# The first three experts of the last pass held in SBUF and loaded in the key pass, with their value chunks split there

## The reference

```
def block(hb):
    qh = (hb @ w_q).reshape(tb, PEER_HEADS, 2, PEER_HALF)
    ...
    best, pos = lax.top_k(cand, PEER_TOPK)
    eidx = jnp.take_along_axis(cidx, pos, axis=-1)
    gates = jax.nn.softmax(best.astype(jnp.float32), axis=-1).astype(hb.dtype)
    act = jax.nn.gelu(jnp.einsum('td,thkd->thk', hb, u_tab[eidx]), approximate=False)
    return jnp.einsum('thk,thkd->td', gates * act, v_tab[eidx])
...
x = x + gt2 * _peer(h2, ...)
return _rmsnorm_2(x, final_norm_w)
```

## Time and profile before

| | us |
|---|---|
| median of 3 runs | 2736.82 |
| lowest, highest | 2735.11, 2752.26 |
| profiled execution | 2736.22 |
| its span | 2734.4 |
| PE busy | 2642.6 (97%) |
| DVE busy | 1921.7 (70%) |
| POOL busy | 1311.6 (48%) |
| ACT busy | 1067.2 (39%) |
| DMA moved | 539.31 MB, mean 197 GB/s |
| key pass in `weigh` | about 1860 to 2171.5 |
| last pass | 2186.9 to 2722 |

### The profile page before, as it was taken

One profiled execution on the slowest core, in us unless ns is written; L12 is line 12 of the kernel. 1 busy time (PEld: TensorE's weight loads), 2 busy tenths in 40 slices (PEclk: granted clock), 3 DMA queues, 4 the chain that ended last, 5 costly groups with the idle time before them and its releaser, 6 DMA issues. The chain is left out here.

```text
span 2734.4 us, 37662 instructions
## 1 busy us (share of the span) xinstructions
PE 2642.6 (97%) x13717; PEld 2229.8 (82%) x13717; DVE 1921.7 (70%) x3096; ACT 1067.2 (39%) x1703; POOL 1311.6 (48%) x622
## 2 busy tenths in 40 slices
PE   8999999999899999999999999999999799999997
PEld 6888887665788887878777899999999788888885
DVE  5445242787854447599776387768999689888897
ACT  4322321455342323352223233335666544444443
POOL 4444452211444445454124467782323368877883
PEclk9999999999999999999899999999999999999998
DMA  5444342112334444332012265558999999999994
GB/s 194 146 143 145 106 166 62 56 54 74 104 123 154 146 138 153 101 110 67 16 63 87 83 179 163 166 157 338 401 392 389 373 359 386 384 385 387 386 387 168
DMA packets 190912, 539.31 MB, mean 197 GB/s; under 512 B 14416, under 2 KB 96464, under 8 KB 170704
## 3 DMA queue, kind: packets, MB, share of 16 engines
q1 hardware_dynamic: 88688, 306.23, 33.6%
q0 software_dynamic: 18432, 134.23, 12.2%
q10 hardware_dynamic: 83680, 97.46, 10.3%
HBM read 482.28 MB, written 55.57 MB: 197 GB/s over the span
## 5 line engine op out<-in xcount | busy, mean ns | idle before, releaser
L358 POOL TENSOR_TENSOR ring_low<-ring,ring_high 128x1024 fp32r<-128x1024 f32 x323 | 801.3, 2482 | 984.4 <-ACT ring_high L318 979.7
L318 ACT ACTIVATE ring_high<-ring 128x1024 fp32r<-128x1024 f32 x354 | 374.2, 1057 | 617.9 <-PE ps L415 485.4
L413 PE MATMUL ps<-u,ring_high 128*128 128x512 f32 (+1 forms) x1504 | 565.8, 376 | 19.6 <-DVE u L520 10.0
L414 PE MATMUL ps<-u,ring_high 128*128 128x512 f32 (+1 forms) x1504 | 559.9, 372 | 0.0
L415 PE MATMUL ps<-u,ring_low 128*128 128x512 f32 (+1 forms) x1504 | 559.7, 372 | 0.0
L358 POOL TENSOR_TENSOR ring_low_more<-ring,ring_high_more 128x1024 fp32r<-128x1024 f32 x103 | 266.8, 2593 | 153.6 <-ACT ring_high_more L318 152.8
L413 PEld LDWEIGHTS ps<-u,ring_high 128*128 128x128 f32 x1504 | 284.0, 189 | 63.4 <-POOL ring_low L641 10.0
L414 PEld LDWEIGHTS ps<-u,ring_high 128*128 128x128 f32 x1504 | 284.2, 189 | 40.1 <-issue 1.4
L415 PEld LDWEIGHTS ps<-u,ring_low 128*128 128x128 f32 x1504 | 284.0, 189 | 39.3
L2867 POOL DMA_INDIRECT fetched_rows<-in_peer_uv,fetch_index x128 | 157.4, 1230 | 180.1 <-DVE ps L2887 138.1
L3487 DVE TENSOR_TENSOR expert_product<-group_acts,group_weights 128x384 f32<-128x384 f32 x128 | 162.9, 1273 | 70.0 <-issue 50.8
(11 more groups left out here) (476 smaller groups left out, 5269.8 us busy)
## 6 DMA issues: line engine op xcount, KB each, us to landing
ring<-in_peer_u SPq DMA_DIRECT2D x128, 512.0 KB
ring<-in_peer_uv SPq DMA_DIRECT2D x128, 512.0 KB
ring<-in_ffn_gu SPq DMA_DIRECT2D x88, 512.0 KB
ada_weights<-in_ada_w SPq DMA_DIRECT2D x48, 512.0 KB, 3.9
ring<-in_ffn_down SPq DMA_DIRECT2D x48, 512.0 KB
expert_acts<-kept_acts ACTq DMA_DIRECT2D x128, 192.0 KB
expert_weights<-weight_stage ACTq DMA_DIRECT2D x24, 1024.0 KB
group_acts<-expert_acts ACTq DMA_DIRECT2D x15, 1536.0 KB
```

The source lines that it names most:

```text
L318: act.activation(k.highs[p], k.ring[:, s], ACT.Copy).then_inc(k.high_ready[p].sem, 1)
L358: pool.tensor_tensor(k.lows[p], k.ring[:, s], k.highs[p].bitcast(F32), ALU.subtract)\
L413: pe.matmul(out, k.highs[p][:, w], high, start=first, stop=False)
L414: pe.matmul(out, k.highs[p][:, w], low, start=False, stop=False)
```

## The change

It makes a class `Edge` for the experts 0, 1 and 2 of the last pass (`EDGE` is now 3). Their activations (3 x 1536 bytes per partition) and gates (24 blocks x 3 experts x 16 tokens) have a place of their own in SBUF at byte 220096, a multiple of 64, where the later products, high and low halves of `combine` lie afterwards. SP loads them in the key pass: the activations and blocks 0 to 17 in front of key chunk 4 of the last round, blocks 18 to 21 behind the first four value chunks; blocks 22 and 23 are copied by ACT out of `weight_stage`. The first four value chunks are all split in the key pass, the low halves on DVE and not on POOL. Products 0 and 1, the rounding of product 0 and its rest also stand in `weigh`. Group 0 without those three experts is loaded in two steps, experts 3 and 4 (semaphore `second`), then 5 to 7. PE's wait for the banks of the key pass is made explicit, per pair of banks. Group 1 is loaded after rounding 3 and not after rounding 1.

```diff
-EDGE = 2
+EDGE = 3
+SECOND = 5
...
+class Edge:
+    AT = 220096
+    SOON = NB - 6
+    def __init__(self, k, ctx, x):
...
+        self.acts = k.nc.alloc_sbuf_tensor_at("edge_acts", [P, EDGE, DT], F32, offset=self.AT)
+        self.weights = k.nc.alloc_sbuf_tensor_at("edge_weights", [P, NB, EDGE * WT], F32, offset=self.AT + EDGE * unit)
...
+    def load_blocks(self, k, sp, lo, hi):
+        for slot in range(2):
+            sp.wait_ge(self.x.staged[slot].sem, 16 * ((hi + 1 - slot) // 2))
+        sp.dma_start(self.weights[:, lo:hi], k.dram["expert_weights"][lo:hi, :, 0:EDGE].rearrange("b p e t -> p b (e t)"))\
+          .then_inc(self.loaded.sem, 16)
+    def load(self, k, sp):
+        for s in range(EDGE):
+            sp.wait_ge(self.x.stored[s].sem, 16)
+        sp.dma_start(self.acts[:], k.dram["expert_acts"][0:EDGE].rearrange("e p t -> p e t")).then_inc(self.loaded.sem, 16)
+        self.load_blocks(k, sp, 0, self.SOON)
+    def copy(self, act):
...
+        for slot in range(2):
+            copy = act.activation(self.weights[:, NB - 2 + slot].rearrange("p (e t) -> p e t", t=WT),
+                                  x.stage[:, slot, 0:EDGE], ACT.Copy)
+    def first(self, dve, n):
+        if n == 0:
+            for b in range(2):
+                dve.wait_ge(self.x.weighed[b].sem, NB)
+            dve.wait_ge(self.loaded.sem, 48)
+            dve.wait_ge(self.copied.sem, 1)
+        if n == 2:
+            dve.wait_ge(self.product_ready.sem, 2)
+        self.multiply(dve, n, self.acts[:, n], self.weights[:, :, n * WT:(n + 1) * WT])
...
 def weigh
-            stream.load(sp)
+            stream.load(sp, midway=lambda: edge.load(k, sp))
+            edge.load_blocks(k, sp, edge.SOON, NB - 2)
...
+                if i == U_ITERS - 1 and e == 6:
+                    edge.copy(act)
...
+                if i == U_ITERS - 1 and e >= 5:
+                    stream.split_high(act, U_ITERS, e - 4)
+                if i == U_ITERS - 1 and e == 6:
+                    edge.round(act, 0)
...
+            edge.first(dve, 0)
+            edge.first(dve, 1)
+            edge.rest(dve, 0)
+            low(8 * U_ITERS + 2)
+            low(8 * U_ITERS + 3)
...
 def combine
-            load_weights(sp, 0, NB - 1, 0, 8, weights_loaded[0])
-            load_acts(sp, 0, 0, EDGE, first_acts)
-            load_acts(sp, 0, EDGE, 8, acts_loaded[0])
+            load_weights(sp, 0, NB - 1, EDGE, SECOND, second)
+            load_acts(sp, 0, EDGE, SECOND, second)
+            load_weights(sp, 0, NB - 1, SECOND, 8, weights_loaded[0])
+            load_acts(sp, 0, SECOND, 8, acts_loaded[0])
...
-                if n == 1:
+                if n == EDGE:
                     for s in range(ACTS):
                         act.wait_ge(x.stored[s].sem, 16 * (P // ACTS))
                     load_acts(act, 1, 0, 8, acts_loaded[1])
```

More of the change, by code:

```diff
@@ L303, in load @@
                     beside(i)
+        if midway is not None:
+            midway()
         for j in range(SLOTS, self.n):
@@ L3206, in v_place, with weigh @@
     return V_PLACES[c - PER_U * U_ITERS]
-def weigh(k, x, choices, acts, block):
+def weigh(k, x, choices, acts, edge, block):
     nc = k.nc
@@ L3429, in coef_high @@
             def coef_high(n):
-                act.wait_ge(product_ready.sem, n + 1)
-                act.activation(high[:, n % WIDE], product[:, n % 3], ACT.Copy).then_inc(high_ready.sem, 1)
+                edge.round(act, n)
                 g = n // 8 + 2
-                if n == 1:
+                if n == EDGE:
                     for s in range(ACTS):
@@ L3451, in _ @@
             copy.then_inc(last_block.sem, 1)
[L3452 to L3455 removed]
+            coef_high(3)
             for n in range(P - WIDE):
@@ L3494, in _ @@
                         x.take_row(dve, c)
-            split(P - 1)
+            edge.rest(dve, P - 1)
             for c in range(CHOICES - 2, CHOICES):
```

104 lines of the change are left out of this document (67 added, 37 removed).

## The result

| | before | after |
|---|---|---|
| median, us | 2735.84 (20 runs, 2728.99 to 2752.26) | 2745.47 (20 runs, 2738.14 to 2753.16) |
| profiled execution | 2736.22, span 2734.4 | 2738.14, span 2736.4 |
| PE busy | 2642.6 | 2656.9 |

The ratio is 1.0033, 95% interval 1.0025 to 1.0042: 9.6 us slower, where 2732.0 and a range to 2742 were forecast. The profiled execution of the changed kernel is the lowest of its 20. It is read first; a second profile of the same kernel, among the experiments, is a usual one.

The account below looks back on a forecast made before the run. The prediction took the DMA engines, through the last group's load, to set the end. Its terms, -1.3 + 1.0 - 3.0 - 1.0 = -4.3 us, took 2736.2 to 2731.9, stated as 2732, with an 8 in 10 range of 2719 to 2742.

Parts of the forecast that it names:

- PE starts expert 63 at 2193.42 + 62 x 4.08 = 2446.4: Last pass before the change: PE at 4.08 us per expert, leaving 7.7 us of margin behind expert 63's remainder.
- They never rest: DMA engines from 2244 to 2633.6: always full, share 1.04 at 386 GB/s, so earlier requests do not bring loads forward.
- Term (d): Long middle of the last pass: 392 instead of 386 GB/s would give 0 to 6.0 us; 1.0 us gain taken.
- Term (c): From 2171.8 to 2244: an earlier start wins back 0 to 7.5 us of lost DMA time; 3.0 us gain taken.
- (a): Last pass: fewer activation bytes and smaller weight pieces at 16 ns each, between -3.6 and +4.2 us; -1.3 us taken.
- (b): Key pass, last round: added activations and 2816 pieces of 192 B carry over 0 to 7.0 us; 1.0 us taken.
- PE would use that up and then wait at each group for the same bytes: Last pass: started 14 us earlier, PE uses up its 7.7 us margin, then waits for loads bound by DMA.
- GpSimd loses three splits in a time when nobody waits for it: Start of the last pass: three splits taken from GpSimd, work queued behind the new waits costed at nothing.
- The start at 2173 that the forecast set aside: Last pass: PE starts at 2173 if engines take queues in turn and small pieces pass in a few us; 2179 taken.
- Rival B: Key pass: small pieces hold up the ring, key chunk 4 late, PE stalls 11 us; 2745 in all; chance 0.12.
- Rival A: Last pass: PE sets the end, loads issued earlier land earlier, the whole start counts; 2719.9; chance 0.14.
- Rival C: Small pieces cost as 512 B ones: 2739.8; signs: under 300 GB/s from 2172 to 2190, last load after 2678; chance 0.13.

Follow-up runs that it names:

- e2: The kernel before with 64 bytes of padding ahead of the last pass's products, high and low halves; 2747.62 us, ratio 1.0042.
- e4: e3 with the weights of all eight experts of group 0 loaded again, in pieces of 512 bytes; 2740.42 us, ratio 1.0017.
- e5: e1 with PE's first matmul of the last pass waiting for the rest of product 3 instead of product 0; 2737.88 us, ratio 1.0008.
- e15: e4 with PE's first matmul of the last pass waiting for the rest of product 2; 2737.18 us, ratio 1.000.
- e1: The changed kernel with Edge.AT 64 bytes lower, so products, high and low halves start at multiples of 128 bytes; 2747.75 us, ratio 1.0041.
- e3: e1 with group 0's weights for experts 3 to 7 in one DMA of 320-byte pieces; 2742.48 us, ratio 1.0015.
- e8: The kernel before with 32 bytes of padding ahead of the high halves and 32 more ahead of the low halves, products unmoved; 2743.30 us, single run.
- e11: e1 with GpSimd writing zeros as the value chunks' low halves in the last pass, without reading SBUF; 2730.32 us, ratio 0.9978.
- e12: The kernel before with GpSimd writing zeros as the value chunks' low halves in the last pass; 2730.12 us, ratio 0.9974.
- e9: e3 with four fetched rows taken out of groups 0 and 1 and put in groups 3, 6, 9 and 12; 2755.79 us, ratio 1.0070.
- e13: e4 with the fetched rows of groups 0 and 1 moved later inside their groups, their number kept; 2747.01 us, ratio 1.003.

## Why the prediction was wrong

- *PE's pace.* The step that failed first is "PE starts expert 63 at 2193.42 + 62 x 4.08 = 2446.4": the duration of a matmul was carried over from before though the change moves its operand. It cost 13.2 us by expert 118, in e2 likewise, and stood in no term and no rival. e2 shows it alone: 12.0 us in the medians.
- *Who sets the end.* "They never rest" was read from a share of 1.04, and the sum was made on the last load as if only bytes counted. The share is 1.04 at 386, 378 and 376 GB/s alike. The last load was issued 7.0 us later (2637.70 for 2630.67), and 10.2 later when counted from the first gate (775.3 for 765.1; 774.4 in the second profile), because its issue stands behind the rounding of product 111 and so follows PE's and VectorE's pace. The landing goes with the issue: where the pace is 4.08 and no stall or moved row comes between (before, e4, e5, e15) it is issued at 764.0 to 765.1 and product 120 comes at 810.9 to 812.3; where it is slower (after twice, e1, e2, e3, e8) at 773.8 to 780.9, and product 120 at 816.0 to 824.2. Term (d), 1.0 us for a middle at 392 GB/s, had the wrong sign for that reason (378). Term (c), 3.0 us for a busier start, won nothing that can be told: in its 72.2 us, laid at the same distance from the first gate, 337 and 352 GB/s in the two profiles of after and 351 before. In terms (a) and (b) the price of 16 ns was near: on average a piece of 128 B took 13 ns and one of 192 B 15 ns in the key pass and 22 in the last pass.
- *The early start is used up by loads.* "PE would use that up and then wait at each group for the same bytes" was right in kind: e11 against e12 shows a gain of nothing from 13.6 us. The place was wrong: not from expert 63 on but within the first eight experts. In after 8.4 us go there (43.2 us from the start to expert 8 instead of 34.8), most of them by value chunk 4 and by the rest that three low splits held, which no term has; group 1's load takes most of it in e11. At an unchanged pace the gain of 4.3 us was some 4 too large as far as kernels without the low halves tell; e4's profile, at 4.080 us with them, ends 1.4 us before the kernel before (867.5 against 868.8), no more than one run differs from the next.
- *What was costed at nothing.* "GpSimd loses three splits in a time when nobody waits for it" holds. But VectorE's lead over PE, 3 to 7 us in groups 1 to 13 before, was not seen as something that the kernel lives on. Without it, the address mended, the same kernel loses 11.7 us by expert 118 (e1); giving the lead back by a late start removes it (e5).
- *The start.* Forecast 8 us sooner, PE at 2179; measured 10.0 and 10.7 sooner, counted from the first gate. The blocks landed in time, product 3 came at 2180.92, forecast 2184, but PE did not keep its clock: expert 0 took 5.82 us, 1.6 over the 4.20 of a later one, where it had been 6.23, 2.1 over 4.08. Of the 2.4 us that were to be won there 0.5 were. The rate of 53 small pieces per us came near for the second edge load (512 pieces in 8.2 us, 63 per us) and not for the first: four fifths of its 2304 passed in 1.8 us. The start at 2173 that the forecast set aside, with the pieces through in a few us, came nearer than 2179. The counts of the earlier trace rows are shares over 8 us and could not decide between the two; how an engine takes its queues in turn no run shows.
- *Rival B* named the time, 2745, by luck and not by its mechanism: PE's last gate matmul is 2.2 to 2.6 us later in the key pass (303.8 and 304.2 against 301.6), not 11. The chain of after shows where:

```profile
2121.15 15.66 DMA ring<-in_peer_u
...
2136.83 1.07 ACT ring_high L320
```

Key chunk 4 is under way for 15.66 us and split at 274.5 from the first gate, against 271.5 before (2137.09 in the earlier trace rows, less 1865.59).
- *Rival A* (the whole start counts, 2719.9) is refuted by e11 and e12, as far as kernels without the low halves tell: there the start is worth nothing. But its mechanism, that a load issued at another time lands at another time, is what the last load shows, in the losing direction. *Rival C* has its price wrong (13 to 22 ns, not 31) and both of its signs came, the first only just: 293 GB/s from 2172 to 2190, and the last load landed behind 2678. The rate around the start of the pass (the 12.2 us above) is low in every profile with the small pieces (223 to 265 GB/s in after twice, e1, e5 and e11, against 335 to 352 in e3, e4, e9, e13 and e15). By e3 and e4 they may be a part of the loss; how much is open, and wide pieces at the old address were not run.

The tail of 56.6 us was right for the profiled execution (56.8 in both profiles).

## What to carry to other kernels

When a change moves a tile, the time of every instruction that reads it is a term of the sum: compare counts over a fixed stretch, since a slower matmul looks like a busy engine. Two engines that hold each other out need a lead between them, and a stall at the head of a pass may be what builds it; before removing a wait, ask what the engine behind it did meanwhile. A DMA share near 1 did not tell here whether bytes set the pace (1.04 at 386 and at 376 GB/s); whether the rate rises when more is asked for tells more.

## What was not expected of the hardware

- A 128x512 fp32 matmul steps at 226.4 ns with stationary tiles at multiples of 128 bytes, at 233.2 with all of them 64 bytes beyond (after, e2), and at 230.8 with high halves 32 and low halves 64 beyond (e8). Weight loads last 188 ns in each of them. Which access is the slow one is open, and so is every other offset.
- With nothing changed but PE's start, the same instructions settle at 4.08 or at about 4.19 us per expert and keep to it for 450 us (e5 and e1). The twelve runs of e3 fall in two lots, five up to 2736.6 and seven from 2742.3 on; which pace a run without a profile had is not known.
- What decides between the two paces is open: leads of 0.1 (e1, e3) and 1.7 us (e4) in group 1 went different ways, but no run set the lead alone.
- A load can move fewer bytes at the same DMA share: 245 GB/s at 1.06 with pieces of 128 and 192 B around the start of the pass, 346 at 1.07 with pieces of 512 B (e4).
